# Layer norm, router and experts put into one stage, with the first two token blocks gathered on TensorE

## The reference

```
x = layer_norm(DN_ALPHA * x + h, ln_g[i, 0], ln_b[i, 0])      # h: the mixer's output
f = moe_ffn(x, w_router, b_router, w_gate[i], w_up[i], w_down[i])
x = layer_norm(DN_ALPHA * x + f, ln_g[i, 1], ln_b[i, 1])

def moe_ffn(x, ...):                                          # 16 experts in 4 groups of 4
    s = sigmoid(x @ w_router);  biased = s + b_router
    grp_score = top_k(biased per group, 2).sum                # sum of the two best of a group
    grp = argmax(grp_score);  top_e = the 2 best experts in that group
    w = s[top_e] / sum(s[top_e]);  gate[token, expert] = w
    h = silu(x @ w_gate) * (x @ w_up) * gate;  return sum over experts of h @ w_down
```

## Time and profile before

| | |
|---|---|
| median of 3 runs | 2393.79 us (2393.79 to 2396.62) |
| the profiled execution | 2399.71 us, its span 2397.9 us |
| busy, share of the span | PE 85%, PEld 72%, DVE 58%, ACT 39%, POOL 5% |
| mean granted clock of TensorE | 0.907 of full speed |
| bytes | 328.30 MB in DMA packets, mean 137 GB/s |
| groups of instructions | L2175 318.8 us busy (x1344), L2333 255.9 us (x112), L2225 213.3 us (x112), L2201 166.8 us (x672) |

### The profile page before, as it was taken

The page is one execution under the profiler, slowest core; times in us unless marked ns, Lnnn a source line. Parts: engine busy times, 40 slices in busy tenths (PEclk is TensorE's granted clock), DMA queues, the critical chain, the costliest instruction groups (busy, mean ns, idle before and its releaser), DMA issues. The chain is left out here.

```text
span 2397.9 us, 29482 instructions
## 1 busy us (share of the span) xinstructions
PE 2038.3 (85%) x11724; PEld 1729.0 (72%) x11724; DVE 1380.2 (58%) x1948; ACT 946.3 (39%) x1376; POOL 125.0 (5%) x184
## 2 busy tenths in 40 slices
PE   5999989979998998999639999299968877479992
PEld 5888879869997876867538887278956666468882
DVE  7864546354654445334339998543056664469995
ACT  4643335121100006234417775221145551357772
POOL 3441000000000000000010000000000000100000
PEclk9999989989999998999759999598889998589996
DMA  7432112232322222211239999313500002279993
GB/s 211 113 68 89 54 53 90 71 80 88 106 75 72 84 71 94 95 46 53 99 124 349 400 391 367 98 57 96 152 6 1 2 1 88 67 266 392 399 395 114
DMA packets 167095, 328.30 MB, mean 137 GB/s; under 512 B 34032, under 2 KB 102432, under 8 KB 166832
## 3 DMA queue, kind: packets, MB, share of 16 engines
q1 hardware_dynamic: 131216, 282.26, 33.3%
q0 software_dynamic: 10144, 28.24, 3.7%
q10 hardware_dynamic: 25600, 15.93, 2.5%
HBM read 301.16 MB, written 19.99 MB: 134 GB/s over the span
## 5 line engine op out<-in xcount | busy, mean ns | idle before, releaser
L2175 PE MATMUL ps<-m_ws,m_xbT 128*128 128x512 f32 x1344 | 318.8, 394 | 2.8 <-DVE m_xbT L2340 2.8
L2175 PEld LDWEIGHTS ps<-m_ws,m_xbT 128*128 128x128 f32 x1344 | 255.3, 190 | 57.1 <-DVE m_xbT L2340 3.6
L2333 DVE TENSOR_TENSOR m_ws<-ring,m_ws 128x2048 fp32r<-128x2048 f32 x112 | 255.9, 2290 | 34.9 <-ACT m_ws L2225 32.8
L1595 PE MATMUL ps<-ffT,ff_ws 128*128 128x264 f32 (+1 forms) x1056 | 241.2, 323 | 4.7 <-DVE ff_ws L423 4.7
L2225 ACT CAST m_ws<-ring 128x2048 fp32r<-128x2048 f32 x112 | 213.3, 1910 | 79.2 <-PE ps L2175 50.8
L1595 PEld LDWEIGHTS ps<-ffT,ff_ws 128*128 128x128 f32 x1056 | 176.4, 190 | 20.4 <-DVE ff_ws L423 4.8
L1595 PE MATMUL ps<-ffT_lo,ff_ws 128*128 128x264 f32 (+1 forms) x528 | 170.1, 322 | 0.0
L2201 PE MATMUL ps<-m_ws,m_hT 128*128 128x512 f32 x672 | 166.8, 397 | 0.0
L2201 PEld LDWEIGHTS ps<-m_ws,m_hT 128*128 128x128 f32 x672 | 122.2, 188 | 23.1
L2330 DVE TENSOR_TENSOR m_ws<-ring,m_ws 128x2048 fp32r<-128x2048 f32 x56 | 128.3, 2290 | 7.7 <-ACT m_ws L2223 6.7
L450 PE MATMUL ps<-fd_ws,fd_xs 128*128 128x512 f32 x528 | 121.6, 393 | 6.7 <-DVE fd_xs L423 6.7
(11 more groups left out here) (491 smaller groups left out, 4262.7 us busy)
## 6 DMA issues: line engine op xcount, KB each, us to landing
ring<-in_moe_w_gate SPq DMA_DIRECT2D x112, 512.0 KB, 5.5
ring<-in_moe_w_up SPq DMA_DIRECT2D x112, 512.0 KB, 7.3
ring<-in_moe_w_down SPq DMA_DIRECT2D x56, 1024.0 KB, 7.9
ring<-in_w_up SPq DMA_DIRECT2D x22, 1024.0 KB, 5.1
ring<-in_w_in SPq DMA_DIRECT2D x16, 1024.0 KB, 6.6
ring<-in_gla_w_in SPq DMA_DIRECT2D x12, 1024.0 KB, 5.3
ring<-in_w_down SPq DMA_DIRECT2D x11, 1024.0 KB, 4.8
ring<-in_nsa_w_in SPq DMA_DIRECT2D x10, 1024.0 KB, 6.9
```

Of the source, the lines that this page charges most:

```text
L1595: ins = nc.tensor.matmul(ps[:, bank, 0:b - a], w[j][:, k, s * P:(s + 1) * P], x[l][:, k, a:b], start=(k == 0 and j == l), stop=(k == KD - ...
L2175: ins = nc.tensor.matmul(ps[:, it % 2, :], xbT[:, blk % 2, a, 4 * half + k, :].bitcast(F32R), v[b][:, k, :], start=(half == 0 and k == 0 a ...
L2333: ins = V.tensor_tensor(o, x.rearrange("p (j k w) -> p j k w", k=4, j=2), x0, ALU.subtract)
```

## The change

1. **No norm stage of its own.** "l0" and "l2" are gone. The residual now also gives the tile's sum (`accum_out`) and its negative mean at once (`residual`), and ACT squares each tile as it comes, in the last part of the mixer's stage (`squares`). The rest of the norm opens the expert stage. Scale and shift are loaded by POOL, during GLA or in `nsa_out`.
2. **Table loads.** A preload of one table set that has both Ln and Exp stands ahead of the squares, in `norm_stage` too; the sigmoid's is also loaded ahead.
3. **The router goes tile by tile**: PE transposes tile t, and multiplies tile t-1 with the router. Slabs 0 and 1 are split in this time, slabs 2 and 3 only behind the gather.
4. **Ranking**: the group's score is the largest of three sums of pairs; experts are ranked after the slots are known. The counts take 5 matmuls in place of 14; the slots take 8 operations of DVE in place of 18 (with the cast).
5. **Blocks 0 and 1** are no longer read back from DRAM: a 0/1 matrix of tokens by slots (`onehot`, 128x256 for each tile) is built on DVE, the normalized rows are split into high and low part (`rh`, `rl`, which lie in the split buffers of slabs 2 and 3), and PE multiplies them: 64 matmuls of 256 columns, for 8 column groups, 2 parts, 4 tiles. 8 more small products give the gates' columns.
6. The rows for the scatter are copied by POOL. The scatter stays, for blocks 2 to 6; blocks 2 and 3 are loaded by ACT in units 1 and 2, after a wait for the scatter. Three tensors' worth of constants come in one load, issued by SP.
7. Semaphores are recycled ahead of `nsa_out` rather than behind it.

```diff
@@ norm_stage, ACT @@
                 if kind:
+                    act.preload_act_table_set("natural_log_exp_and_others")
                     act.wait_ge(epsset, 2)
@@ Program @@
+    def residual(self, link, t, new, done, centred):
+        st, y = self.lst, self.h[:, t, :].rearrange("p (a c) -> p a c", a=2)
+        link(self.nc.vector.scalar_tensor_tensor(y, y, ALPHA, new, ALU.mult, ALU.add, accum_out=st[:, 3, t:t + 1]))
+        self.nc.vector.tensor_scalar(st[:, 4, t:t + 1], st[:, 3, t:t + 1], -1 / D, None, ALU.mult).then_inc(centred, 1)
+    def squares(self, act, junk, centred, squared):
+        for t in range(TT):
+            act.wait_ge(centred, t + 1)
...
+            self.nc.scalar.activation(junk, self.h[:, t, :], ACT.Square, bias=self.lst[:, 4, t:t + 1],
+                                      accum_out=self.lst[:, 0, t:t + 1]).then_inc(squared, 1)
@@ moe_stage, PE @@
+                for t in range(TT + 1):
+                    if t < TT:
+                        pe.wait_ge(normed, t + 1)
...
+                            ins = nc.tensor.transpose(ps[:, b, P * (k % 4):P * (k % 4) + P], h[:, t, k * P:(k + 1) * P], self.ident[:])
...
+                    u = t - 1
+                    if u >= 0:
+                        pe.wait_ge(evac, 2 * u + 2)
+                        for k in range(KD):
+                            ins = nc.tensor.matmul(ps[:, 4, NE * u:NE * (u + 1)], xT[:, k, P * u:P * (u + 1)], wr[:, k, :],
...
+                nc.tensor.matmul(ps[:, 5, 0:20], before, gsel[:], start=True, stop=False)
+                for d in range(1, TT + 1):
+                    ins = nc.tensor.matmul(ps[:, 5, 4 * d:20], ones[:], gsel[:, 0:20 - 4 * d], start=False, stop=(d == TT))
...
+                pe.wait_ge(rl_done, TT)
+                pe.wait_ge(hot, TT)
+                for k in range(KD):
...
+                    for a in range(2):
+                        for t in range(TT):
+                            ins = nc.tensor.matmul(ps[:, xbank[k], 256 * a:256 * a + 256], (rh, rl)[a][:, t, k * P:(k + 1) * P].bitcast(F32R),
+                                                   onehot[:, t].bitcast(F32R), start=(t == 0), stop=(t == TT - 1))
...
+                        if it == 0:
+                            pe.wait_ge(gate_done, 1)
+                            for b in range(2):
+                                for t in range(TT):
+                                    ins = nc.tensor.matmul(ps[:, 4, EG * b:EG * b + EG], onehot[:, t, P * b:P * b + P], rows[:, t, D:XROW],
@@ moe_stage, ACT @@
+                act.wait_ge(squared, TT)
+                link(nc.scalar.activation(lst[:, 1], lst[:, 0], ACT.Ln, bias=self.lneps[:], scale=1 / D))
+                nc.scalar.activation(lst[:, 2], lst[:, 1], ACT.Exp, scale=-0.5).then_inc(rs, 1)
...
+                        if u in (1, 2):
+                            load_x(u + 1)
@@ moe_stage, POOL @@
+                for t in range(TT):
+                    pool.wait_ge(normed, t + 1)
+                    nc.gpsimd.tensor_copy(rows[:, t, 0:D].rearrange("p (k q) -> p k q", k=KD),
+                                          h[:, t, :].rearrange("p (q k) -> p k q", k=KD)).then_inc(rows_in, 1)
...
+                pool.wait_ge(gate_done, 1)
                 pool.wait_ge(slot_done, 1)
@@ moe_stage, DVE @@
+                for t in range(TT):
+                    dve.wait_ge(rh_done, t + 1)
+                    V.tensor_tensor(rl[:, t].bitcast(F32R).rearrange("p (k q) -> p k q", k=KD), h[:, t, :].rearrange("p (q k) -> p k q", k=KD),
...
+                lo(0)
+                lo(1)
...
+                for t in range(TT):
+                    V.tensor_scalar(onehot[:, t].bitcast(F32R), slots, slotf[:, t:t + 1], None, ALU.is_equal).then_inc(hot, 1)
```

More of the change, by code:

```diff
@@ new lines, in _ @@
+                act.preload_act_table(ACT.Sigmoid)
+                act.wait_ge(lg_done, 1)
+                nc.scalar.activation(s[:], ps[:, 4, 0:TT * NE], ACT.Sigmoid).then_inc(s_out, 1)
+                for k in range(KD):
+                    act.wait_ge(xp_done, k + 1)
+                    nc.scalar.copy(xbT[:, :, :, k, :].rearrange("p b a c -> p a b c").bitcast(F32R),
+                                   ps[:, xbank[k], :].rearrange("p (a b c) -> p a b c", a=2, b=2)).then_inc(xp_out, 1)
+                hi(2)
@@ L2365, in _ @@
[L2365 to L2368 removed]
+                V.reduce_sum(rows[:, :, D:XROW], gate[:].rearrange("p (t g e) -> p t e g", t=TT, g=NGRP), AX.X).then_inc(gate_done, 1)
+                link(V.tensor_scalar(gidf[:], blockno, extra[:, 1:2], None, ALU.is_ge))
@@ L2429, in _ @@
             def _(sp):
+                for to, frm in loads:
+                    sp.dma_start(to, frm).then_inc(loaded, 16)
                 W.send(sp)
```

252 lines of the change are left out of this document (151 added, 101 removed).

## The result

| | before | after |
|---|---|---|
| median | 2395.2 us (2393.79 to 2396.88, 4 runs) | 2318.5 us (2316.17 to 2319.83, 4 runs) |
| the profiled execution | 2399.71 us, span 2397.9 | 2316.17 us, span 2314.4 |
| mean granted clock | 0.907 | 0.927 |
| PE, PEld, DVE, ACT, POOL busy | 85, 72, 58, 39, 5% | 88, 75, 60, 41, 6% |

The ratio is 0.9678, with an interval of 0.9662 to 0.9695: faster by 76.7 us.

What follows compares the result with a forecast made beforehand. The prediction took the chain from last residual to first expert product, 87.8 us in the first layer, as the bound. 39.9 + 37.7 + 5.3 = 82.9 us off 2399.71 gives 2316.8; the median 5.9 lower, 2311 us (range 2297 to 2331).

Steps and rivals of the forecast that it cites:

- norm's start: From last residual to first scaling: 10.3 us shrink to 3.1 us, with DVE's accumulator taken as free; -7.2 us.
- norm, router, first splits: From scaling to ranking: overlap tile by tile makes it 27.1 us for 31.3; -4.2 us.
- slots to first product: From slots to first expert product: a gather of 64 products takes 9.8 us instead of 29.7; -19.9 us.
- in the experts: Within the experts: warm start -2.8, gate products +1.9, block 1's transposes gone -1.0, slabs split late +2.0 us.
- other norms: Norms "l1", "l3" and "n2": two table loads go and one preload comes; -2.0, -2.0 and -1.3, together -5.3 us.
- POOL's copies I put at 0.7: In the norm: POOL's row copies cost 0.7 us, as only the second tile's scaling is on PE's path.
- Scaling longer than 1.28 us: In the norm: a scaling operation over 1.28 us was listed as a sign that the forecast is wrong.
- POOL holds DVE: Rival, 10%, in the norm: every POOL copy holds DVE for its 2.1 us, 4 us a layer, 2318 us.
- Late slabs +2.0: In the experts: slabs 2 and 3, split only behind the gather, fit with little to spare; +2.0 us allowed.
- low through the whole gather: Rival, 12%: the clock stays low through the gather and into unit 0; 12.5 us less gain, 2323 us.
- the 6% rival: Rival, 6%: the clock rises within the router, making it 3.5 us shorter a layer, 2304 us.
- The scatter never stopped ACT: Rival, 2%, behind unit 1: ACT waits for the scatter and the experts stop; 2412 us if it lasts 85 us.

Runs made afterwards that it cites:

- after_again: The changed kernel run once more, unedited, as yardstick: 2316.7 us.
- old_rank: The changed kernel with the ranking of the kernel before put back: 2327.1 us.
- dram_gather: The changed kernel with only the gather undone: the first two blocks go through the slots in DRAM as in the kernel before; 2352.6 us.
- no_preload: The changed kernel without the early table load in the norms of their own stage: 2323.3 us.
- pool_late: The changed kernel with only GpSimd's four copies of the token rows moved, to wait until the 0/1 rows are written: 2311.6 us.
- both_late: The changed kernel with both GpSimd's row copies and the low parts of slabs 0 and 1 moved behind the slots: 2319.5 us.
- warm_router: As act_rows_warm, plus fill products with unused results on PE ahead of and within the router: 2292.2 us.
- act_rows_warm: The changed kernel with slabs 0 and 1's low parts behind the slots, fill products while PE waits behind router and counts, row copies on ScalarE: 2304.8 us.
- lo_late: The changed kernel with only the low parts of slabs 0 and 1 moved from ahead of the bias sum to behind the slot numbers: 2310.3 us.

## Why the prediction was right, and where it was not

The forecast was 2311 us (2297 to 2331); it came to 2318.5. The terms sum to 82.9 us against the profiled execution, and 83.5 were measured between the two profiled ones. By the medians the gain was 76.7 us, and 78.9 beside after_again: 4 to 6 us less than the terms. The forecast set the median 5.9 us under the profiled execution before; it lay 4.5 us under it, and the profiled one after lay 2.3 us under its own median. There is one trace of the kernel before, so it stays open how much of the terms measured below belongs to that one execution. The terms, first layer:

| term | forecast | measured |
|---|---|---|
| norm's start | -7.2 | -7.6 (11.6 to 4.0) |
| norm, router, first splits | -4.2 (to 27.1) | -1.8 (31.3 to 29.5) |
| ranking | -3.9 | -4.0 |
| counts | -3.8 | -3.8 |
| slots | -1.0 | -1.0 |
| slots to first product | -19.9 | -20.7 (29.7 to 9.0) |
| in the experts | +0.1 | -1.9 |
| first layer | -39.9 | -40.8 |
| second layer | -37.7 | -38.7 (-38.0 ahead of the experts, -0.7 in them) |
| other norms | -5.3 | -5.6 (2.1, 2.1, 1.3) |

**What held.** Norm's start: DVE's accumulator is read in 0.08 us and was taken as nothing. Ranking, counts and slots by so many operations of so long: each within 0.1 us, and old_rank gives the same 3.8 us when the ranking alone is put back. The gather: 64 products with the clock rising in it, 9.0 us for 9.8; dram_gather shows that the term is real and that nothing had hidden the way through DRAM. The three other norms: no_preload gives the size back, and there is no gap behind a table load. (A norm has one table load where it had two; the forecast's signs say "two loads of tables fewer a norm", its sum has one.)

The measured terms add up to 85.1 us, 1.6 more than came out between the two profiled executions; those were lost outside these stages.

**The step that failed** is "norm, router, first splits", 27.1 us where 29.5 came, and in it one size: "POOL's copies I put at 0.7". The forecast priced them on PE's path, where only the second tile's scaling stands. They held DVE's norm for 5.3 us and the tokens' second low part for another 1.8 (3.80 us instead of 2.04, at 1181.18), and all four tiles count, since DVE is the chain. "Scaling longer than 1.28 us", one of the forecast's own signs of being wrong, did come. pool_late shows what the rest of the term was worth: without the copies beside it the bias sum comes at 26.2 us, against the 26.4 that the forecast has without its 0.7. So the copies cost 3.5 and 3.2 us up to the bias sum (after_again against pool_late), 5.1 us by the medians for both layers. The rival "POOL holds DVE" (10%), a copy's whole time for each tile, 4 us a layer and 2318 us, is what happened. That the sum of the terms still came out within 1 us is luck: the experts gave 2.0 us more a layer than forecast and the gather 0.8 (first layer). The tokens' low parts took 2.04 us where 1.7 were taken.

**"Late slabs +2.0" did not come.** The experts' other three terms, -2.8, +1.9 and -1.0, make the -1.9 that was measured. PE idles 0.6 us of 243 in the changed kernel. How near it was, both_late shows: there the next loads start 4 us later behind the first product, the scatter later too, and the experts last 5.0 to 5.6 us longer.

**The other rivals.** The clock was not low through the whole gather. It did not rise within the router here, though the 6% rival was a true possibility: it did so for the first two tiles of one layer in two later executions, and warm_router, which makes it happen, gains 6.4 us over act_rows_warm's first layer. The scatter never stopped ACT: it was issued at 1205.9 and ACT issued the load behind unit 1 at 1228.7 without idle time.

## What to carry to other kernels

Ask of a chain which engine is in it after the change, not before: here the work that had been cover (DVE's splits, ACT's rounding) had become the chain, so two lines moved behind it (lo_late) brought 6.4 us. A copy given to GpSimd is not free beside DVE, and short operations of DVE pay the most; look which of its results then come late and what waits for them (in both_late the split of a slab, and behind it the weight loads). And a stretch of small products on PE can be worth filling with useless large ones: look at the granted clock in it first.
